# Three 256-column matmuls per weight tile, summed in one half bank of PSUM, in place of a 512-column and a 256-column one

## The chip, the cores and the metric

The kernel runs on one core of a Trainium2 chip. The metric is the device time of one execution in microseconds. The engines named below are PE (TensorE, matmuls; its weight loads have a row of their own, PEld), DVE (VectorE), ACT (ScalarE) and SP (SyncE, which here only issues DMAs). PSUM is the memory that PE writes: 8 banks of 512 fp32 columns on 128 partitions. SBUF is the memory that all engines read.

## What is computed

Two transformer-like blocks on one sequence of 256 tokens and width 2048, all in fp32:

```python
h = rmsnorm(x, g_mix)
z = h @ w_in                                  # cb, cc, cv, q, k, v, f, gate_c, gate_a
conv_y = cb * causal_dwconv(cc * cv, conv_w)
attn = forgetting_attention(q, k, v, log_f)   # 8 heads of 128
merged = sigmoid(gate_c + b) * (conv_y @ w_conv_out) + sigmoid(gate_a + b) * (attn @ w_attn_out)
x = x + merged @ w_mix_out
x = x + square(relu(rmsnorm(x, g_mlp) @ w_ff1)) @ w_ff2
x = rmsnorm(x, g_final)
# second block
q, k, v, p = split(rms_norm(x, g) @ w_in_2)
a = moba_attention(rms_norm(q), rms_norm(k), v, rel_bias)
m = multiscale_pool(p, pool_w, pool_scale)    # four products of 256 x 256
x = x + concat(a, m) @ w_out_2
x = x + (silu(gate) * val) @ w_down_2         # gate, val: conv(rms_norm(x) @ w_up_2)
```

With 256 tokens the work is the reading of 446 MB of weights and the matmuls on them.

## The kernel before, in words

**Precision.** Every fp32 operand of a large product is held as two numbers of type fp32r, a high part and the rest: a weight as WH and WL, an activation in a buffer of 16 K-blocks (XHL, MHL; AHL and CHL have 8) whose 512 columns are 256 tokens of high part, then 256 tokens of low part. A product is high x high + high x low + low x high.

**Weights** come by DMA in units of 1024 columns of 128 partitions (RAW, issued on SP), ACT rounds each to WH (L840), DVE subtracts to WL (L1279). There are five buffers of each, and both engines run up to four units ahead of PE.

**Items.** The program is one list of items that all engines walk in the same order. Three kinds matter here:

- *features* items (q, k, cc, cv, cb, the gates, conv, attn, ff, Q, K, pool, up gate, up val): the result has features on the partitions. The weight tile of 128 x 128 is the stationary operand and the activation the moving one. An item is 4 tiles wide and up to 16 K-blocks deep. For a K-block and a pair of tiles `j0`, `j0 + 1` PE does (L684) the two high weights against all 512 activation columns, then (L686) the two low weights against the 256 high columns. Each tile has a bank of its own: columns 0 to 255 collect high x high + low x high, columns 256 to 511 collect high x low.
- *tokens* items (v, the residual products) and *group* items (most of w_ff2 and w_down): the activation is stationary, the weight moves, three matmuls of 512 columns on one bank (`three`, L717 to L719). Groups have also seven-product steps (`sevens`), in which DVE builds sums of weights and activations.
- *small products* (transposes, scores, probabilities x values, head norms, row spreads, the two pooled products) are put between the parts of an item, at places written out by hand in the plan.

**PSUM.** The eight banks are two sides of four. Items take sides in turn; `take` makes PE wait until what was on the side has been read out. A small product goes to the side that the running item does not use, and is noted in the same `free` list.

**Evacuation.** A features item's two column halves are in PSUM; `fold` adds them: ACT copies the high x low half of all four banks to TA (L894), DVE adds the other half (L1363), and only then comes the step that the item is for, on TA: multiply by the row of norm factors RB (L1375, L1387, L1510, L1753, L1765) or by a gate. Each of these is a stage of a queue (`Pending`) that is pumped twice between two weight splits, so a stage stands behind a WH or WL split. Who may overwrite TA is kept in ACT's `free["TA"]`.

Of the kernel before, what the change touches and what calls it, by code (L numbers as in the profile page):

```python
# [5 lines left out]
P = 128  # L6
T = 256
# [83 lines left out]
class Part:  # L91
# [3 lines left out]
    banks: list  # L95
# [5 lines left out]
class Item:  # L101
# [4 lines left out]
    side: int = 0  # L106
    mid: dict = field(default_factory=dict)
# [5 lines left out]
    args: dict = field(default_factory=dict)  # L113

# [26 lines left out]
class Plan:  # L141
# [102 lines left out]
    def second_half(self):  # L244
# [12 lines left out]
        for i in range(2):  # L257
            at = POOL_AT[i]
            parts = self.tokens(w2, 0, ALLK[:at], 2048 + 512 * i)
            side = self.turn ^ 1  # L260
# [5 lines left out]
            small = Item("pooled", ("pooled", i), pool, ("M", "pools"), side, args={"i": i})  # L266
# [25 lines left out]
def build(nc, io):  # L292
# [5 lines left out]
    with ctx:  # L298
# [87 lines left out]
        def signals(names):  # L386
# [8 lines left out]
        hi, x_hi, part_hi, sum_hi, copied, squared, root, gate, tap, exps, probs, placed, softplus, cr_hi, pair1, rooted, act_step = (  # L395
            signals("hi x_hi part_hi sum_hi copied squared root gate tap exps probs placed softplus cr_hi pair1 rooted act_step"))

        lo, t_made, x_lo, summed, summing, left, evacuated, scaled, multiplied, tapped, mean, column, diagonal, row = (
            signals("lo t_made x_lo summed summing left evacuated scaled multiplied tapped mean column diagonal row"))
# [129 lines left out]
        def tensor(e):  # L529
# [3 lines left out]
            free = [None, None]  # L533

            def take(s):
                if free[s]:
                    own.wait_ge(*free[s][0][free[s][1]])
                return 4 * s

# [4 lines left out]
            def first(s, u):  # L544
# [11 lines left out]
                if u == 7:  # L556
                    free[1] = x_lo, ("mix", 15)

            def vec(s):
                b = take(s)  # L560
# [5 lines left out]
                free[s] = row_in, "vec"  # L566

            def rel(s):
                b = take(s)
                own.wait_ge(s_rel, rel_all)  # L570
                mm(PS[0:8, b, 0:384], RELT[:], OH[:, 0:384], start=True, stop=True).then_inc(*own.made(rel_up, "rel"))
                free[s] = row_in, "er"

            def spread(s, key):
                b = take(s)
# [4 lines left out]
                free[s] = row, key  # L580

            def log_f(s):
                b = take(s)
# [5 lines left out]
                free[s] = logit, "z"  # L589

            def running(s):
                b = take(s)
# [6 lines left out]
                free[s] = row_in, "cr"  # L599

            def score(s, block, h):
                b = take(s)
# [15 lines left out]
                free[s] = masked, (block, h)  # L618

            def turn(s, block, h):  # L620
                b = take(s)
# [5 lines left out]
                free[s] = probs, (block, h)  # L627

            def mix(s, block, h):
                vv, _ = ATT[block]  # L630
                b = take(s)
# [7 lines left out]
                free[s] = mixed, (block, h)  # L639

            def turn_x(s, of, g):
                b = take(s)
# [7 lines left out]
                free[s] = x_lo, (of, 4 * g + 3)  # L650

            def head_norm(s, key):
                sq = SQA if key[0] == "Q" else SQB
                b = take(s)
# [4 lines left out]
                free[s] = norm_left, key  # L659

            def pooled(s, it):
                features(it)

            small_products = {"first": first, "vec": vec, "rel": rel, "spread": spread, "log f": log_f, "running": running,
                              "scores": score, "turn": turn, "mix": mix, "turn x": turn_x, "head norm": head_norm,
                              "pooled": pooled}

            def between(it, n):
                for what, *args in it.mid.get(n, ()):
                    if what in small_products:  # L670
                        small_products[what](it.side ^ 1, *args)

            def features(it):
                b, x = take(it.side), BUF[it.src[0]]
                for n, p in enumerate(it.parts):
                    own.wait_ge(*lo[p.ent])
                    h, l = wview(WH, p.ent), wview(WL, p.ent)
                    for k, kc in enumerate(p.kcs):
# [3 lines left out]
                        for j0 in range(0, len(p.banks), 2):  # L682
                            for j in (j0, j0 + 1):
                                mm(PS[:, b + p.banks[j], :], h[:, k, j * P:(j + 1) * P], x[:, kc, :], start=st, stop=False)  # L684
                            for j in (j0, j0 + 1):
                                t = mm(PS[:, b + p.banks[j], 0:T], l[:, k, j * P:(j + 1) * P], x[:, kc, 0:T],  # L686
                                       start=False, stop=en)
                    t.then_inc(*own.made(used, p.ent))
                    between(it, n)
                free[it.side] = left, it.key  # L690

            def gates(it):
                b, (p,) = take(it.side), it.parts
# [4 lines left out]
                free[it.side] = evacuated, "f"  # L698

            def tokens(it):  # L700
                b, x = take(it.side), BUF[it.src[0]]
# [12 lines left out]
                free[it.side] = (placed, it.key) if it.kind == "v" else (evacuated, it.key)  # L714
# [6 lines left out]
            def group(it):  # L721
                b, x = take(it.side), MHL
                sevens = [n for n, st in enumerate(it.steps) if st.seven]
                for n, st in enumerate(it.steps):
# [22 lines left out]
                    if o:  # L747
                        bp = take(it.side ^ 1)
# [13 lines left out]
                    if c:  # L762
                        free[it.side ^ 1] = left, it.key
                last = {"out": (stored, (it.args["g"], 1, 1)), "final group": (evacuated, ("final", 1))}
                free[it.side] = last.get(it.kind, (evacuated, it.key))
# [6 lines left out]
            first(1, 0)  # L772
            zeros(WARM // 2)
            first(1, 1)
# [29 lines left out]
        ROW = {"proj": "r1", "cc": "r1", "cv": "r1", "cb": "r1", "gate": "r1", "ff": "r2", "qk": "r3", "pool": "r3"}  # L804
        SPREADS = [None, "r1", "r2", "r3", "r4"]
        SPREAD_SIDE = {args[0]: it.side ^ 1 for it in items for mids in it.mid.values() for what, *args in mids
# [6 lines left out]
        def wide_ps(it, lo_, hi_):  # L813
            return PS[:, 4 * it.side:4 * it.side + 4, lo_:hi_]

        def scalar(e):
# [71 lines left out]
            def fold(it):  # L888
                own.wait_ge(*used[it.end])
                if free["TA"]:  # L890
                    s, key = free["TA"]
                    own.wait_ge(*s[key])
                chain()
                e.copy(TA[:], wide_ps(it, T, 2 * T)).then_inc(*own.made(copied, it.key))  # L894
                yield
# [11 lines left out]
            def proj(it):  # L907
                yield from fold(it)
                free["TA"] = evacuated, it.key
# [16 lines left out]
            def running():  # L926
                own.wait_ge(*run_up["run"])
                b = 4 * (item_of["cc", 0].side ^ 1)
# [34 lines left out]
            def mix(s, block, h):  # L963
# [3 lines left out]
                act(dst[:, 4 * h:4 * h + 4, 0:T], PS[:, 4 * s:4 * s + 4, 0:T], AF.Copy).then_inc(  # L967
# [15 lines left out]
            def cc(it):  # L983
                yield from fold(it)
                free["TA"] = evacuated, it.key
                yield

            def cv(it):
                yield from fold(it)
                yield from nothing(2)  # L990
                free["TA"] = multiplied, it.key
                yield from taps(TB[:, :, 0:T], it.key, 4 * it.args["half"], False)

            def cb(it):
                yield from fold(it)
                yield from nothing(2)
                split_product(CHL, 4 * it.args["half"], it.key, multiplied)
                free["TA"] = evacuated, it.key

            def gates(it):  # L1000
                yield from fold(it)
                yield
                g, half = it.args["g"], it.args["half"]
                own.wait_ge(*scaled[it.key])
# [4 lines left out]
                free["TA"] = scaled, it.key  # L1009
                yield  # L1010

            def conv(it):
                yield from fold(it)
                free["TA"] = evacuated, it.key
                yield

            def attn(it):
                yield from fold(it)
                yield from nothing(2)
                split_product(MHL, 4 * it.args["g"], it.key, multiplied)  # L1020
                free["TA"] = evacuated, it.key

            def turn_x(s, of, g):
                for n in range(2):
                    if n == 0:
                        own.wait_ge(*turned[of, g])
                    split_bank(of, 4 * g + 2 * n, PS[:, 4 * s + n, :])
# [20 lines left out]
            def ff(it):  # L1048
                yield from fold(it)
# [897 lines left out]
```

## Time and profile before

| | us |
|---|---|
| median of 3 runs | 2383.57 (2383.52 to 2384.89) |
| the profiled execution | 2383.46 |
| its span, first to last instruction | 2381.6 |

| engine | busy us | share of the span | instructions |
|---|---|---|---|
| PE | 2376.9 | 100% | 12581 |
| PEld | 2035.4 | 85% | 12581 |
| DVE | 1700.7 | 71% | 1804 |
| ACT | 1216.5 | 51% | 1427 |

A matmul's recorded duration holds the time that it drains through the array, while the next already streams; what one costs in a row of them is the distance from its start to the next start, or its piece in the chain of waits. Each matmul has a weight load of its own, also where the stationary operand is that of the matmul before.

### The profile page before, as it was taken

To read this page: it belongs to the slowest core of one execution; us is meant where nothing else is said; L and a number is where in the kernel's file an instruction comes from. 1 tells how busy PE (TensorE), PEld (TensorE's weight loads), DVE (VectorE), ACT (ScalarE), POOL (GpSimd) and SP (SyncE) were. 2 spreads that over 40 slices of the span, in tenths; PEclk is the share of its full clock that TensorE was granted. 3 is DMA by queue.
4 is the path that set the end of the run, shared out by engine and by line. 5 is a ranking of instruction groups with operands and counts; after the bars stand their busy time and mean duration, and the time that the engine had idled before them with its cause. 6 is when DMAs were issued, how large, how long until landed. Compare 5 with 4: busy or idle time off the path is not lost.

```text
span 2381.6 us, 30785 instructions
## 1 busy us (share of the span) xinstructions
PE 2376.9 (100%) x12581; PEld 2035.4 (85%) x12581; DVE 1700.7 (71%) x1804; ACT 1216.5 (51%) x1427; POOL 0.2 (0%) x4
## 2 busy tenths in 40 slices
PE   9999999999999999999999999999999999999999
PEld 8888888888888888888888888888888888888887
DVE  6565666666568868868768667855778778886788
ACT  5444454554545445445445555555555455545554
POOL 0000000000000000000000000000000000000000
PEclk9999999999999999999999999999999999999999
DMA  7566556666555665655665565555655665566655
GB/s 253 160 187 196 167 185 196 191 188 196 186 187 178 219 216 189 213 181 198 202 190 193 182 185 160 171 183 186 186 181 194 196 192 176 186 219 186 188 173 181
DMA packets 238040, 452.15 MB, mean 190 GB/s; under 512 B 16569, under 2 KB 20779, under 8 KB 237771
## 3 DMA queue, kind: packets, MB, share of 16 engines
q1 hardware_dynamic: 237147, 449.07, 59.3%
q8 instruction: 99, 1.62, 0.3%
q10 hardware_dynamic: 752, 1.12, 0.1%
q14 instruction: 42, 0.34, 0.0%
HBM read 446.46 MB, written 3.67 MB: 189 GB/s over the span
## 4 chain that ended last, share of the span: by engine, by line
PE 97%; DVE 2%; ACT 0%; issue 0%; ACTq 0%; DVEq 0%
PE PS L684 41%; PE PS L686 21%; PE PS L717 11%; PE PS L718 11%; PE PS L719 11%; DVE WL L1279 1%; PE PS L648 0%; PE PS L615 0%; PE PS L636 0%; PE PS L657 0%; ACT WH L840 0%; PE PS L542 0%; PE PS L625 0%; DVE PB L1259 0%; PE PS L553 0%
## 5 line engine op out<-in xcount | busy, mean ns | idle before, releaser
L1279 DVE TENSOR_TENSOR WL<-RAW,WH 128x1024 fp32r<-128x1024 f32 (+1 forms) x844 | 1002.0, 1204 | 520.6 <-ACT WH L840 519.1
L684 PE MATMUL PS<-XHL,WH 128*128 128x512 f32 x3968 | 1248.9, 396 | 0.0
L840 ACT ACTIVATE WH<-RAW 128x1024 fp32r<-128x1024 f32 (+1 forms) x845 | 867.5, 1041 | 744.4 <-PE PS L686 478.3
L686 PEld LDWEIGHTS PS<-XHL,WL 128*128 128x128 f32 x3968 | 745.4, 188 | 176.0
L686 PE MATMUL PS<-XHL,WL 128*128 128x256 f32 x3968 | 779.7, 278 | 0.0
L684 PEld LDWEIGHTS PS<-XHL,WH 128*128 128x128 f32 x3968 | 605.1, 189 | 2.1 <-issue 1.0
L717 PE MATMUL PS<-WH,MHL 128*128 128x512 f32 x1000 | 390.2, 390 | 0.0
L719 PE MATMUL PS<-WH,MHL 128*128 128x512 f32 x1000 | 389.2, 389 | 0.0
L718 PE MATMUL PS<-WL,MHL 128*128 128x512 f32 x1000 | 389.1, 389 | 0.0
L719 PEld LDWEIGHTS PS<-WH,MHL 128*128 128x128 f32 x1000 | 187.7, 188 | 39.3
L717 PEld LDWEIGHTS PS<-WH,MHL 128*128 128x128 f32 x1000 | 187.7, 188 | 38.8 <-issue 0.3
L718 PEld LDWEIGHTS PS<-WL,MHL 128*128 128x128 f32 x1000 | 187.8, 188 | 38.0
L905 ACT ACTIVATE MHL<-TA 128x1024 fp32r<-128x1024 f32 x33 | 35.0, 1062 | 120.4 <-DVE TA L1600 61.9
L1363 DVE TENSOR_TENSOR TA<-TA,PS 128x1024 f32<-128x1024 f32 x72 | 87.9, 1221 | 3.7 <-ACT TA L894 1.2
L894 ACT COPY TA<-PS 128x1024 f32<-128x1024 f32 x72 | 73.3, 1018 | 13.5 <-DVE K L1694 3.3
L1380 DVE TENSOR_TENSOR MHL<-TA,MHL 128x1024 fp32r<-128x1024 f32 x33 | 40.5, 1226 | 28.0 <-ACT MHL L905 26.7
L840 ACT ACTIVATE WH<-PB 128x1024 fp32r<-128x1024 f32 x24 | 25.4, 1058 | 56.1 <-DVE PT L1271 43.6
L717 PE MATMUL PS<-WH,XHL 128*128 128x512 f32 x128 | 50.2, 392 | 0.0
L718 PE MATMUL PS<-WL,XHL 128*128 128x512 f32 x128 | 49.9, 390 | 0.0
L719 PE MATMUL PS<-WH,XHL 128*128 128x512 f32 x128 | 49.8, 389 | 0.0
L684 PE MATMUL PS<-AHL,WH 128*128 128x512 f32 x128 | 40.2, 395 | 0.0
L684 PE MATMUL PS<-CHL,WH 128*128 128x512 f32 x128 | 40.2, 395 | 0.0
(212 smaller groups left out, 1374.6 us busy)
## 6 DMA issues: line engine op xcount, KB each, us to landing
RAW<-in_w_ff SPq DMA_DIRECT2D x256, 512.0 KB, 4.1
RAW<-in_w_in SPq DMA_DIRECT2D x224, 512.0 KB, 3.9
RAW<-in_w_up SPq DMA_DIRECT2D x176, 512.0 KB, 4.1
RAW<-in_w_down SPq DMA_DIRECT2D x88, 512.0 KB, 4.4
RAW<-in_w_mix_out SPq DMA_DIRECT2D x32, 512.0 KB, 4.0
RAW<-in_w_out SPq DMA_DIRECT2D x32, 512.0 KB, 3.7
RAW<-in_w_conv_out SPq DMA_DIRECT2D x16, 512.0 KB, 3.7
RAW<-in_w_attn_out SPq DMA_DIRECT2D x16, 512.0 KB, 4.3
```

The costliest lines, as they stand in the source:

```text
L684: mm(PS[:, b + p.banks[j], :], h[:, k, j * P:(j + 1) * P], x[:, kc, :], start=st, stop=False)
L686: t = mm(PS[:, b + p.banks[j], 0:T], l[:, k, j * P:(j + 1) * P], x[:, kc, 0:T], start=False, stop=en)
L717: mm(PS[:, bank, :], xh, h, start=first, stop=False)
L718: mm(PS[:, bank, :], xh, l, start=False, stop=False)
L719: return mm(PS[:, bank, :], xl, h, start=False, stop=last)
L840: act(high, raw, AF.Copy).then_inc(*own.made(hi, i))
L894: e.copy(TA[:], wide_ps(it, T, 2 * T)).then_inc(*own.made(copied, it.key))
L905: act(dst[:, c0:c0 + 4, 0:T], TA[:], AF.Copy).then_inc(*own.made(part_hi, key))
L1279: tt(low, raw, high.bitcast(f32), sub).then_inc(*own.made(lo, i))
L1363: tt(TA[:], TA[:], wide_ps(it, 0, T), add).then_inc(*own.made(left, it.key))
L1380: tt(dst[:, c0:c0 + 4, T:2 * T], TA[:], dst[:, c0:c0 + 4, 0:T].bitcast(f32), sub).then_inc(*own.made(evacuated, key))
```

## The change

In features items each weight tile and K-block now has three matmuls of 256 columns on the same 256 columns of PSUM: high weight x high activation, high weight x low activation, low weight x high activation. The four tiles of an item are four quarters of two banks, so an item takes the first two banks of its side ("front"). The `start` flag stands at a bank's first quarter alone. `fold` is gone on ACT and DVE; the step that the item is for reads PSUM directly (`product`, `four`).

The other two banks of the side ("back") take the small products that are put into the item; scores and the transposes of the probabilities, which need four banks, stay on the other side. `take` becomes `front_of`, `back_of` and `all_of`, with a list each. `mix` packs its four heads into two banks. The pooled products go to the back banks of their own item, and are read from PSUM. ACT no longer writes TA at an item's start; where it does later (`up gate`, `up val`, `pool`, `head norm`) it waits first (`may_write_ta`). DVE gets one new wait: in the second gate item it waits for ACT's sigmoid of the first (`gate["gc", g]`) ahead of writing TA. DMAs, weight splits, tokens and group items keep their instructions.

```diff
@@ features, PE
-                b, x = take(it.side), BUF[it.src[0]]
+                b, x = (back_of(it.side) if it.base else front_of(it.side)), BUF[it.src[0]]
...
-                        for j0 in range(0, len(p.banks), 2):
-                            for j in (j0, j0 + 1):
-                                mm(PS[:, b + p.banks[j], :], h[:, k, j * P:(j + 1) * P], x[:, kc, :], start=st, stop=False)
-                            for j in (j0, j0 + 1):
-                                t = mm(PS[:, b + p.banks[j], 0:T], l[:, k, j * P:(j + 1) * P], x[:, kc, 0:T],
-                                       start=False, stop=en)
+                        for j, q in enumerate(p.quarters):
+                            o = PS[:, b + q // 2, T * (q % 2):T * (q % 2) + T]
+                            mm(o, h[:, k, j * P:(j + 1) * P], x[:, kc, 0:T], start=st and q % 2 == 0, stop=False)
+                            mm(o, h[:, k, j * P:(j + 1) * P], x[:, kc, T:2 * T], start=False, stop=False)
+                            t = mm(o, l[:, k, j * P:(j + 1) * P], x[:, kc, 0:T], start=False, stop=en and q % 2 == 1)
...
-                free[it.side] = left, it.key
+                if it.kind == "pooled":
+                    back[it.side] = pool_in, 4 * it.args["i"] + 3
+                else:
+                    front[it.side] = OUT_OF_PSUM.get(it.kind, left), it.key
@@ fold, ACT
-                e.copy(TA[:], wide_ps(it, T, 2 * T)).then_inc(*own.made(copied, it.key))
@@ fold, DVE
-                tt(TA[:], TA[:], wide_ps(it, 0, T), add).then_inc(*own.made(left, it.key))
+            def product(it):
+                chain()
+                own.wait_ge(*used[it.end])
+                return four(it.bank)
@@ up val, DVE
-                yield from fold(it)
-                chain()
-                tt(TC[:, :, 2:258], TA[:], over4(RB[:]), mul).then_inc(*own.made(multiplied, it.key))
+                tt(TC[:, :, 2:258], product(it), over4(RB[:]), mul).then_inc(*own.made(multiplied, it.key))
@@ gates, DVE
+                if it.args["half"]:
+                    own.wait_ge(*gate["gc", it.args["g"]])
@@ mix, PE
-                    mm(PS[:, b + i, 0:T], vv[:, 0, c:c + P], PT[:, i, 0:T], start=True, stop=False)
-                    t = mm(PS[:, b + i, P:T], vv[:, 1, c:c + P], PT[:, i, T:384], start=False, stop=True)
+                    o = PS[:, b + i // 2, T * (i % 2):T * (i % 2) + T]
+                    mm(o, vv[:, 0, c:c + P], PT[:, i, 0:T], start=True, stop=False)
+                    t = mm(o[:, P:T], vv[:, 1, c:c + P], PT[:, i, T:384], start=False, stop=True)
```

PE's instructions around the transposes of the first attention's probabilities (L625 before, L638 after; both are `turn`, PB the probabilities, CONST the identity), before:

```order
L684 MATMUL PS<-XHL,WH 128x512 x2
L686 MATMUL PS<-XHL,WL 128x256 x2
L625 MATMUL PS<-CONST,PB 128x128 x12
L684 MATMUL PS<-XHL,WH 128x512 x2
L686 MATMUL PS<-XHL,WL 128x256 x2
```

and after the change:

```order
L703 MATMUL PS<-XHL,WL 128x256
L638 MATMUL PS<-CONST,PB 128x128 x12
L701 MATMUL PS<-XHL,WH 128x256
L702 MATMUL PS<-XHL,WH 128x256
L703 MATMUL PS<-XHL,WL 128x256
L701 MATMUL PS<-XHL,WH 128x256
L702 MATMUL PS<-XHL,WH 128x256
```

Four matmuls for two tiles (1536 columns) become six (1536 columns); the small product stands at the same place.

DVE at the last `up val` item, ahead of the seven-product step of the last group; L1363 is the fold, L1765 the multiplication by RB, L1497 and L1503 the convolution's taps, L1259 to L1271 the weight sums of the seven-product step. Before:

```order
L1363 TENSOR_TENSOR TA<-TA,PS 128x1024
L1765 TENSOR_TENSOR TC<-TA,RB 128x4x256
L1279 TENSOR_TENSOR WL<-RAW,WH 128x1024
L1497 SCALAR_TENSOR_TENSOR TA<-TC,VEC,TA 128x256 x4
L1279 TENSOR_TENSOR WL<-RAW,WH 128x1024
L1503 SCALAR_TENSOR_TENSOR TA<-TC,VEC,TA 128x256 x4
L1769 TENSOR_TENSOR TA<-TA,TB 128x1024
```

and after:

```order
L1279 TENSOR_TENSOR WL<-RAW,WH 128x1024 x6
L1750 TENSOR_TENSOR TC<-PS,RB 128x4x256
L1279 TENSOR_TENSOR WL<-RAW,WH 128x1024
L1496 SCALAR_TENSOR_TENSOR TA<-TC,VEC,TA 128x256 x4
L1502 SCALAR_TENSOR_TENSOR TA<-TC,VEC,TA 128x256 x4
L1279 TENSOR_TENSOR WL<-RAW,WH 128x1024
L1754 TENSOR_TENSOR TA<-TA,TB 128x1024
```

One instruction of 1024 columns is gone and the multiplication reads PSUM; one weight split has moved from between the taps to behind them.

## Rows read from the trace of the kernel before

**Rows 1.** The page: engines' busy time, and their busy tenths over time.

```profile
PE 2376.9 (100%) x12581; PEld 2035.4 (85%) x12581; DVE 1700.7 (71%) x1804; ACT 1216.5 (51%) x1427; POOL 0.2 (0%) x4
...
PEclk9999999999999999999999999999999999999999
```

**Rows 2.** The page's chain that ended last: shares of the span.

```profile
PE 97%; DVE 2%; ACT 0%; issue 0%; ACTq 0%; DVEq 0%
```

**Rows 3.** Groups by line and shape: count | busy us, mean ns | idle before.

```profile
L684 PE MATMUL PS<-XHL,WH 128*128 128x512 f32 x3968 | 1248.9, 396 | 0.0
...
L1363 DVE TENSOR_TENSOR TA<-TA,PS 128x1024 f32<-128x1024 f32 x72 | 87.9, 1221 | 3.7 <-ACT TA L894 1.2
L894 ACT COPY TA<-PS 128x1024 f32<-128x1024 f32 x72 | 73.3, 1018 | 13.5 <-DVE K L1694 3.3 <-DVE Q L1694 2.5 <-DVE MHL L1380 2.5
...
L684 PE MATMUL PS<-AHL,WH 128*128 128x512 f32 x128 | 40.2, 395 | 0.0
...
L684 PE MATMUL PS<-CHL,WH 128*128 128x512 f32 x128 | 40.2, 395 | 0.0
...
L684 PE MATMUL PS<-MHL,WH 128*128 128x512 f32 x16 | 5.0, 394 | 0.0
```

**Rows 4.** Chain that ended last, 300 to 480 us: share of the stretch by line.

```profile
by line: PE PS L684 67.0%; PE PS L686 33.1%
```

**Rows 5.** The same stretch: busy us (count), of L686, then of L684 alone.

```profile
300.00:480.00 180.00, 101.45 (x517) 97.15 (x518) 1.00 0.62 192
...
300.00:480.00 180.00, 162.31 (x518) 1.00 0.62 192
```

**Rows 6.** Weight loads of features items in order of time: start us, us.

```profile
900.37 0.42 PEld L686 LDWEIGHTS PS<-XHL,WL 128*128 128x128 f32 x2
900.72 0.30 PEld L684 LDWEIGHTS PS<-XHL,WH 128*128 128x128 f32 x2
```

**Rows 7.** Chain pieces in features items and a `mix` block: start us, us.

```profile
152.05 0.43 PE PS L636 x2
152.49 0.22 PE PS L637 x2
152.71 0.46 PE PS L684 x2
153.17 0.23 PE PS L686 x2
```

**Rows 8.** Longest chain pieces: runs of one kind of matmul: start us, us.

```profile
58.45 3.71 PE PS L696 x16
...
132.04 1.31 PE PS L625 x12
```

**Rows 9.** Chain shares in a group item, 2330 to 2370 us, then L718's count.

```profile
by line: PE PS L717 33.5%; PE PS L719 33.5%; PE PS L718 33.4%
...
2330.00:2370.00 40.00, 22.95 (x59) 10.96 (x60) 1.00 0.57 192
```

**Rows 10.** Who the weight loads waited for: us in total, times, longest.

```profile
PEld PS L717 <- DVE WL L1279: 1.1, 2, 0.6
...
PEld PS L717 <- DVE TA L1363: 0.5, 1, 0.5
```

**Rows 11.** PE matmuls, then weight loads, at one such wait: start us, us.

```profile
2080.88 0.39 PE L719 MATMUL PS<-WH,AXL 128*128 128x512 f32 x1
2081.38 0.50 PE L717 MATMUL PS<-WH,AXH 128*128 128x512 f32 x1
...
2081.94 0.39 PE L719 MATMUL PS<-WH,AXL 128*128 128x512 f32 x1
...
2081.38 0.19 PEld L717 LDWEIGHTS PS<-WH,AXH 128*128 128x128 f32 x1 [0.54 <-DVE WL L1279]
2081.48 0.19 PEld L718 LDWEIGHTS PS<-WL,AXH 128*128 128x128 f32 x1
```

**Rows 12.** DVE before that wait and at 61 us: start us, us.

```profile
2055.14 1.22 DVE L1363 TENSOR_TENSOR TA<-TA,PS 128x1024 f32<-128x1024 f32 x1
...
60.90 1.22 DVE L1363 TENSOR_TENSOR TA<-TA,PS 128x1024 f32<-128x1024 f32 x1
```

More of the change, by code:

```diff
@@ L113, with bank @@
     args: dict = field(default_factory=dict)
+    @property
+    def bank(self):
+        return 4 * self.side + self.base
     @property
@@ L556, in first @@
                 if u == 7:
-                    free[1] = x_lo, ("mix", 15)
+                    front[1] = back[1] = x_lo, ("mix", 15)
             def vec(s):
-                b = take(s)
+                b = back_of(s)
                 own.wait_ge(s_const, 16)
@@ L579, in spread @@
                 t.then_inc(*own.made(spread_up, key))
-                free[s] = row, key
+                back[s] = row, key
             def log_f(s):
-                b = take(s)
+                b = back_of(s)
                 own.wait_ge(*evacuated["f"])
@@ L617, in score @@
                 t.then_inc(*own.made(scores, (block, h)))
-                free[s] = masked, (block, h)
+                front[s] = back[s] = masked, (block, h)
             def turn(s, block, h):
-                b = take(s)
+                b = all_of(s)
                 own.wait_ge(*normed["P", block, h])
@@ L626, in turn @@
                 t.then_inc(*own.made(probs_up, (block, h)))
-                free[s] = probs, (block, h)
+                front[s] = back[s] = probs, (block, h)
             def mix(s, block, h):
                 vv, _ = ATT[block]
-                b = take(s)
+                b = back_of(s)
                 own.wait_ge(*probs[block, h])
@@ L713, in tokens @@
                     between(it, i)
-                free[it.side] = (placed, it.key) if it.kind == "v" else (evacuated, it.key)
+                front[it.side] = (placed, it.key) if it.kind == "v" else (evacuated, it.key)
             def three(bank, xh, xl, h, l, first, last):
@@ L762, in group @@
                     if c:
-                        free[it.side ^ 1] = left, it.key
+                        front[it.side ^ 1] = back[it.side ^ 1] = left, it.key
                 last = {"out": (stored, (it.args["g"], 1, 1)), "final group": (evacuated, ("final", 1))}
-                free[it.side] = last.get(it.kind, (evacuated, it.key))
+                front[it.side] = back[it.side] = last.get(it.kind, (evacuated, it.key))
             own.wait_ge(*zero_made["zero"])
@@ L886, in columns2, with may_write_ta, fresh @@
                 yield
[L888 to L892, printed above, removed]
-                chain()
-                e.copy(TA[:], wide_ps(it, T, 2 * T)).then_inc(*own.made(copied, it.key))
-                yield
+            def may_write_ta():
+                s, key = free["TA"]
+                own.wait_ge(*s[key])
+            def fresh(it):
                 if it.key in FRESH:
@@ L1086, in qk @@
             def qk(it):
-                yield from fold(it)
-                free["TA"] = evacuated, it.key
+                yield from fresh(it)
                 yield
@@ L1201, in parts @@
                             work.flush()
-                            g = pooled(args[0])
-                            next(g)
-                            work.later(g)
+                            work.later(pooled(args[0]))
             free["EV"] = None
@@ L1762, in up_val @@
                 g = it.args["g"]
-                yield from fold(it)
-                chain()
-                tt(TC[:, :, 2:258], TA[:], over4(RB[:]), mul).then_inc(*own.made(multiplied, it.key))
+                tt(TC[:, :, 2:258], product(it), over4(RB[:]), mul).then_inc(*own.made(multiplied, it.key))
                 yield
@@ L1828, in parts @@
                             work.flush()
[L1829 to L1831 removed]
+                            work.later(pooled(args[0]))
             e.memset(ZERO, 0.0).then_inc(*own.made(zero_made, "zero"))
```

248 lines of the change are left out of this document (112 added, 136 removed).

## The prediction

> **What bounds the kernel now.** I read the page first. PE is busy all through the span at the full granted clock, while DVE has 29% and ACT 49% of it to spare [rows 1], and the chain that ended last is 97% matmuls [rows 2]. So the time is the sum of what each matmul takes of PE's stream, plus the few places where PE waits. What one takes is not its recorded 396 ns [rows 3], which counts the drain too; it is the piece that it has in the chain. I took a stretch of 180 us that holds features items alone. There the 512-column matmuls are 67.0% of the chain and the 256-column ones 33.1% [rows 4], with 518 and 517 of them [rows 5]: 0.670 x 180 / 518 = 232.8 ns and 0.331 x 180 / 517 = 115.24 ns. The single pieces agree: 0.46 and 0.23 us for two [rows 7]. A weight tile and K-block costs one of each, 348.06 ns. There are 3968 + 128 + 128 + 16 = 4240 of them [rows 3], 1476 us of the span.
>
> **The matmuls.** The change takes away 4240 matmuls of 512 columns and adds 8480 of 256. The columns stay the same, 768 for a tile and K-block; matmuls and weight loads grow from two to three. If each of the three takes what the 256-column ones take now, a tile and K-block costs 3 x 115.24 = 345.7 ns, 2.34 less, and all of them 2.34 x 4240 = 9.9 us less. The shares are rounded to 0.1%, which is up to 0.5 ns here, so 2 us either way.
>
> Why should a 256-column matmul keep its 115 ns when no long ones stand around it? Three things could end that.
>
> Weight loads: a load starts together with the matmul ahead of it, not earlier. Two loads that stand beside 256-column matmuls fit into 0.30 us although each lasts 0.19, so the second begins some 0.11 us behind the first [rows 6]. After a stall two loads of the same kind start 0.10 us apart [rows 11]. The load is therefore no longer than the 115 ns that it has to hide under, and since none is drawn further ahead now, the present pairs of 256s are already in the state in which all would be: of the four loads of a pair of tiles, two lie under a 256-column matmul. The bound from below is the run of 12 transposes, each with a load of its own: 1.31 / 12 = 109 ns [rows 8]. The bound from above comes from the group items, below (120.5 ns). I take 115.24, since it is the same instruction on the same buffers.
>
> PSUM: three matmuls in a row now add to the same 256 columns, 115 ns apart; before, neighbours were on different banks. In `mix`, the second matmul of each head adds to the columns that the first wrote 0.43 / 2 / 2 = 0.11 us earlier, and it takes 0.22 / 2 = 0.11 us, as a transpose of 128 columns does [rows 7, 8]. Nothing for it, then. If the adder did stall, each matmul would show more than 115 ns, which is the same rival as the next.
>
> Instructions: PE gets two (load, matmul) in 115 ns, without a pause. The longest run at such a rate is 12 pairs [rows 8], so whether the supply holds for 192 pairs of a whole item isn't shown. Nothing for it, with the price in the rival.
>
> **The fold.** 72 copies of 1.018 us on ACT and 72 additions of 1.221 us on DVE [rows 3]. 73 and 88 us leave two engines that are not the bound, so all of it is hidden except where PE waits for them. The multiplication that now reads PSUM is of the same 1024 columns as the addition that read PSUM (1.22 us), and takes that one's place in the queue. PE waited three times for a DVE result for over 0.3 us: twice for a weight sum's low part in a seven-product step, once for the fold itself [rows 10]. At the first of the two, three matmuls took 2081.94 - 2080.88 = 1.06 us in place of 3 x 0.227 = 0.68, so 0.38 us are lost [rows 11]; DVE's chain up to there had begun with a fold at 2055.14 [rows 12]. A chain shorter by 1.2 us removes a wait of 0.38: 2 x 0.38 = 0.8 us less. What is late next there is the landing and splitting of the units behind, for which I have no row and count nothing. The third, at the first v item, stays: DVE did the fold at 60.90, behind other work [rows 12], and will do k's multiplication at that moment.
>
> **PSUM sides and waits.** A features item's front is free when its first read of PSUM is done; that is one DVE instruction after the item's end, before it was a copy and an addition, and the side is wanted only an item later (22 us for 16 K-blocks). Small products in the back banks wait for the small product before them, where they used to wait for an evacuation as well. `scores` and the transposes still wait for the other side, whose item ended at least two parts earlier. Bounds: no gain, since no row shows PE waiting there; no loss, since each wait is for something no later than before. Zero. The new wait on DVE (second gate item, for a sigmoid of the item before): behind it are DVE's weight splits, for which PE waits; but the sigmoids come a whole item earlier. Zero. The pooled products lose a fold: hidden.
>
> **A rule against the change.** The rows give 232.8 ns for 512 columns and 115.24 for 256, so more than twice for twice the columns, no fixed cost per matmul. The Trainium skill, page "TensorE: Matmul & The Clock Gate", section "Back-to-back issue gap", gives columns / 2.4 + 2.5 ns for a warm matmul, a small fixed cost: by it a third matmul is 2.5 ns more for each tile and K-block, an estimate of 10.6 us more in all, 2394 us. The same rule would put the present pair at 325 ns, where the rows have 348.
>
> **The sum.** 2383.46 (the profiled execution; the median of the runs is 2383.57) - 9.9 - 0.8 = 2372.8 us, 0.45% less.
>
> **Rivals.**
>
> *Each matmul costs a fixed amount (slower).* In a group item a 512-column matmul takes 0.335 x 40 / 59 = 227.1 ns [rows 9]. At 2.4 GHz 512 columns stream in 213.3, which leaves 13.8. In features items 348.06 - 320 = 28.1 for two matmuls, 14.0 each: nearly the same, which speaks for a cost per matmul, paid somewhere in the pair and not where the starts show it. Then a 256-column matmul costs 106.7 + 13.8 = 120.5 ns, three cost 361.4, 13.3 more, and the kernel takes 2383.46 + 56.6 - 0.8 = 2439 us. Against it: the starts in features items are 0.23 us apart for two 256s and 0.46 for two 512s, every time, and 16 matmuls of 512 columns with a stationary operand of only 16 columns still take 3.71 / 16 = 232 ns each [rows 8], so the rate seems to belong to the columns that stream. The point at which it decides is 116.0 ns a matmul (348.06 / 3), not one ns above what I count on. A supply of instructions that doesn't keep up, or a stall in PSUM's adder, ends here too. Chance 0.22, anywhere from 2388 to 2440.
>
> *Staying on one bank is quicker (faster than forecast).* Groups stay on a bank for three matmuls and have 227.1 ns, features change banks and have 232.8. If that is the cause, 256 columns cost 115.24 x 227.1 / 232.8 = 112.4 ns, three 337.3, and the kernel takes 2383.46 - 45.8 - 0.8 = 2337 us. At the transposes' 109 ns it would be 2383.46 - 86.8 - 0.8 = 2296. Against it: the 16 matmuls just named are on one bank and have 232. Chance 0.10.
>
> *Nothing changes.* The two weight loads of the same tile may weigh as the long matmul did, or the 256s come out at 115.5 to 116.5 ns instead of 115.24: 2379 to 2388 us. The forecast is only 2.34 ns a tile, so a small error in it lands here. Chance 0.13.
>
> **Chances.** The forecast's own case, 114.6 to 115.5 ns a matmul, 2364 to 2379 us: 0.55. A measurement here can tell about 0.2%, 4.8 us. Faster by more: 0.55 + 0.10 = 0.65, less 0.04 for its upper edge, 0.61. Slower by more: 0.22. The rest, 0.17, is no change. A range from 2355 to 2440 leaves out the quicker case, 0.10, and what little would be above 2440.
>
> **What the profile after would show.** In a stretch of features items the three lines have a third of the chain each, 115 ns a matmul, and the stretch of an item of 16 K-blocks is 22.1 us. Over 116.0 ns, and evenly on all three lines, is the fixed cost. More on the second and third line than on the first is PSUM's adder. Weight loads that start later than their matmul's predecessor would show the instruction supply. ACT's busy time falls to 1143 us, DVE's to 1613; the waits for L1279's weight sums are gone. I am wrong if PE waits at item starts or small products for a bank, or if the group and tokens items, which nothing touches, change their 227 ns.

## Result: 2438.17 us, 2.3% slower

| | before | after |
|---|---|---|
| median of runs, us | 2383.55 | 2438.17 (2437.67 to 2438.70, 4 runs) |
| ratio | | 1.0228, 95% interval 1.021 to 1.0246 |
| span of the profiled execution | 2381.6 | 2436.8 |
| granted clock | full | full |

I had forecast 2372.8 us. The change costs 54.6 us where I counted on a gain of 11. The rival "each matmul costs a fixed amount" had 2439 us.

The page of the changed kernel, in answer to [rows 1] and [rows 2]:

```profile
PE 2427.0 (100%) x16821; PEld 2273.0 (93%) x16821; DVE 1616.5 (66%) x1732; ACT 1142.7 (47%) x1355; POOL 0.2 (0%) x4
...
PE 96%; DVE 2%; ACT 1%; issue 0%; DMA 0%; ACTq 0%; DVEq 0%
```

PE has 4240 matmuls and 4240 loads more. ACT has lost what was forecast (1143 us), DVE nearly (1613). Together they have 3% of the chain, so the gain on them is worth next to nothing.

The chain of waits in a stretch of features items alone, 310 to 480 us, and the count of L701 there (L702 and L703 have 473 too), in answer to [rows 4] and [rows 5]:

```profile
by line: PE PS L703 33.4%; PE PS L701 33.4%; PE PS L702 33.3%
...
310.00:480.00 170.00, 133.66 (x473) 1.00 0.59 182
```

0.334 x 170 / 473 = 120.0 ns for each of the three lines, where I had counted on 115.24. A tile and K-block takes 360 ns and not 345.7. In order of time, PE's matmuls and then its weight loads (start us, us; compare [rows 6]):

```profile
400.01 0.28 PE L702 MATMUL PS<-XHL,WH 128*128 128x256 f32 x1
400.13 0.28 PE L703 MATMUL PS<-XHL,WL 128*128 128x256 f32 x1
400.25 0.28 PE L701 MATMUL PS<-XHL,WH 128*128 128x256 f32 x1
...
400.02 0.19 PEld L703 LDWEIGHTS PS<-XHL,WL 128*128 128x128 f32 x1
400.14 0.19 PEld L701 LDWEIGHTS PS<-XHL,WH 128*128 128x128 f32 x1
400.26 0.19 PEld L702 LDWEIGHTS PS<-XHL,WH 128*128 128x128 f32 x1
```

Some 98% of the starts in features items are exactly 120 ns behind the one before, on all three lines alike. The group items have kept their 227 ns.

The extra 11.9 ns (360 - 348.06) on 4240 tiles and K-blocks are 50.6 us. The rest, some 4 us, is waiting: by the starts, PE now stands five times, together 5.3 us longer than ordinary steps, where it stood twice for 0.6 us together. Who the weight loads and the matmuls waited for (us, times, longest), in answer to [rows 10]:

```profile
PEld PS L736 <- DVE WL L1279: 2.2, 3, 1.2
...
PE PS L701 <- DVE WL L1279: 2.8, 2, 1.4
```

I had said that the waits for L1279 would be gone; there are five of them now where there were two, and longer ones. The first, in order of time (compare [rows 11]):

```profile
2050.99 0.28 PE L703 MATMUL PS<-XHL,WL 128*128 128x256 f32 x1
2052.68 0.35 PE L701 MATMUL PS<-XHL,WH 128*128 128x256 f32 x1 [1.41 <-DVE WL L1279]
```

1.69 us from start to start where a step is 0.12.

### The profile page after: what moved, and what is told of

Read it like the earlier page. It is cut to its first block, busy times and chain, and to the rows that moved or that the text cites. A ratio compares the mean times of both kernels' runs of the same rounds, so it can differ in the third digit from the quotient of the medians.

```text
span 2436.8 us, 39061 instructions
## 1 busy us (share of the span) xinstructions
PE 2427.0 (100%) x16821; PEld 2273.0 (93%) x16821; DVE 1616.5 (66%) x1732; ACT 1142.7 (47%) x1355; POOL 0.2 (0%) x4
## 4 chain that ended last, share of the span: by engine, by line
PE 96%; DVE 2%; ACT 1%; issue 0%; DMA 0%; ACTq 0%; DVEq 0%
PE PS L701 20%; PE PS L703 20%; PE PS L702 20%; PE PS L736 11%; PE PS L738 11%; PE PS L737 11%; DVE WL L1279 1%; PE PS L662 0%; ACT WH L862 0%; PE PS L628 0%; PE PS L650 0%; PE PS L671 0%; PE PS L638 0%; ACT TA L994 0%; DVE TA L1502 0%
## 5 line engine op out<-in xcount | busy, mean ns | idle before, releaser
L1279 DVE TENSOR_TENSOR WL<-RAW,WH 128x1024 fp32r<-128x1024 f32 (+1 forms) x844 | 1002.4, 1205 | 690.6 <-ACT WH L862 688.0
L862 ACT ACTIVATE WH<-RAW 128x1024 fp32r<-128x1024 f32 (+1 forms) x845 | 865.3, 1041 | 859.4 <-PE PS L703 569.3
L701 PE MATMUL PS<-XHL,WH 128*128 128x256 f32 x3968 | 1125.8, 284 | 2.8 <-DVE WL L1279 2.8
L703 PE MATMUL PS<-XHL,WL 128*128 128x256 f32 x3968 | 1122.8, 283 | 0.0
L702 PE MATMUL PS<-XHL,WH 128*128 128x256 f32 x3968 | 1122.8, 283 | 0.0
L701 PEld LDWEIGHTS PS<-XHL,WH 128*128 128x128 f32 x3968 | 761.5, 192 | 4.6 <-issue 4.0
L702 PEld LDWEIGHTS PS<-XHL,WH 128*128 128x128 f32 x3968 | 761.6, 192 | 0.5
L703 PEld LDWEIGHTS PS<-XHL,WL 128*128 128x128 f32 x3968 | 761.5, 192 | 0.0
L924 ACT ACTIVATE MHL<-TA 128x1024 fp32r<-128x1024 f32 x33 | 35.0, 1061 | 99.8 <-DVE TA L1754 65.6
L862 ACT ACTIVATE WH<-PB 128x1024 fp32r<-128x1024 f32 x24 | 25.4, 1059 | 56.0 <-DVE PT L1271 43.5
L736 PE MATMUL PS<-WH,AXH 128*128 128x512 f32 x96 | 37.7, 393 | 1.1 <-DVE WL L1279 1.1
L994 ACT ACTIVATE TB<-TC,VEC 128x256 f32<-128x256 f32 x44 | 22.9, 591 | 32.7 <-DVE TC L1740 32.7
```

Of the source, the lines that this page charges most:

```text
L701: mm(o, h[:, k, j * P:(j + 1) * P], x[:, kc, 0:T], start=st and q % 2 == 0, stop=False)
L702: mm(o, h[:, k, j * P:(j + 1) * P], x[:, kc, T:2 * T], start=False, stop=False)
L703: t = mm(o, l[:, k, j * P:(j + 1) * P], x[:, kc, 0:T], start=False, stop=en and q % 2 == 1)
L736: mm(PS[:, bank, :], xh, h, start=first, stop=False)
L862: act(high, raw, AF.Copy).then_inc(*own.made(hi, i))
L924: act(dst[:, c0:c0 + 4, 0:T], TA[:], AF.Copy).then_inc(*own.made(part_hi, key))
```

## Experiments

Theory F: a matmul on fp32r operands costs its columns at 2.4 GHz and a fixed 13 to 14 ns, so the third matmul is what the change costs; the 233 and 115 ns between starts before the change don't show the cost of each. Theory S: what waiting there is comes from the stage that went with the fold (a stage is one entry of the queue that ACT and DVE work off between two weight splits). Times of single executions are compared with 2383.5 to 2383.7 us of the kernel before on the same chip. "Per tile" below is ns of one weight tile and one K-block, from the starts in the trace with the small joints at the ends of items in it (before: 348.5, after: 360.5 when counted so).

### Only the split, in the kernel before

```diff
-                                mm(PS[:, b + p.banks[j], :], h[:, k, j * P:(j + 1) * P], x[:, kc, :], start=st, stop=False)
+                                w = h[:, k, j * P:(j + 1) * P]
+                                mm(PS[:, b + p.banks[j], 0:T], w, x[:, kc, 0:T], start=st, stop=False)
+                                mm(PS[:, b + p.banks[j], T:2 * T], w, x[:, kc, T:2 * T], start=False, stop=False)
```

> The kernel before, with one edit: each 512-column matmul of a features item becomes two of 256 columns, on the same bank and the same columns as before. Fold, banks and sides stay as before. Theory F (each matmul costs its columns at 2.4 GHz and some 13.5 ns more, whatever its length): all 256-column matmuls are 120 ns apart, a tile and K-block goes from 348 to 360 ns, and the time from 2383.5 to about 2433 us. Rival P (the changed kernel is slow because three matmuls in a row add to the same PSUM columns): here only two of them are on the same columns and not in a row, so they keep 115 ns and the time is 2373 us. Rival R (something else in the change, evacuation or banks, slows PE): 2383 us or less.

2432.5 us, 48.9 more than before. Its page and its chain from 320 to 480 us:

```profile
PE 2424.9 (100%) x16821; PEld 2271.5 (93%) x16821; DVE 1701.3 (70%) x1804; ACT 1217.4 (50%) x1427; POOL 0.2 (0%) x4
...
by line: PE PS L686 33.4%; PE PS L685 33.4%; PE PS L688 33.3%
```

DVE and ACT still have the fold, four banks are in use, no three matmuls in a row are on the same columns, and the three lines have a third of the chain each, at 120 ns. This one edit holds 48.9 of the 54.6 us. P and R are out.

### Two banks in turns, in the changed kernel

```diff
+                            for c in range(2):
+                                for w, lo_ in ((h, 0), (h, T), (l, 0)):
+                                    for q in (c, c + 2):
...
+                                        t = mm(o, w[:, k, q * P:(q + 1) * P], x[:, kc, lo_:lo_ + T],
```

> The changed kernel, with the matmuls of two tiles taken in turns (tile q and q + 2, whose quarters lie in different banks), so that no matmul adds to the columns of the one before it. Same matmuls, same sums. Theory F: 120 ns a matmul still, 2438 us. Rival P (PSUM's adder on the same columns): back to about 115 ns, 3 x 5 x 4240 = 64 us less, 2375 us.

2437.5 us, 120 ns. Adding to the columns of the matmul before costs nothing that shows, and loading the same tile twice in a row (here there is another between) isn't what costs either.

### Runs of eight, in the kernel before

```diff
-                        for j0 in range(0, len(p.banks), 2):
-                            for j in (j0, j0 + 1):
-                                mm(PS[:, b + p.banks[j], :], h[:, k, j * P:(j + 1) * P], x[:, kc, :], start=st, stop=False)
-                            for j in (j0, j0 + 1):
-                                t = mm(PS[:, b + p.banks[j], 0:T], l[:, k, j * P:(j + 1) * P], x[:, kc, 0:T],
...
+                    for k, kc in enumerate(p.kcs):
+                        for j, bank in enumerate(p.banks):
+                            mm(PS[:, b + bank, :], h[:, k, j * P:(j + 1) * P], x[:, kc, :],
...
+                    for k, kc in enumerate(p.kcs):
+                        for j, bank in enumerate(p.banks):
+                            t = mm(PS[:, b + bank, 0:T], l[:, k, j * P:(j + 1) * P], x[:, kc, 0:T],
...
```

> The kernel before, with the matmuls of a unit (two K-blocks, four tiles) in another order: eight of 512 columns, then eight of 256, where it had two and two. Same matmuls. Theory F: the time stays at 2383.5 us within 3 us (16 matmuls still take 2787 ns); and if the starts only show a shifted picture of a fixed cost, the later ones of the run of eight are 227 ns (512 columns) and 120 ns (256 columns) apart, not 233 and 115. Rival C (the cost lies in the columns, 232.8 and 115.2 ns, and something else makes 120 of it in the changed kernel): 233 and 115 ns all through both runs.

2387.9 us, 4.2 more; per tile 349.3. The chain's pieces (start us, us):

```profile
400.24 0.95 PE PS L687 x8
401.19 1.84 PE PS L683 x8
403.03 0.95 PE PS L687 x8
```

0.95 / 8 = 119 and 1.84 / 8 = 230 ns, not 115 and 233. By the starts, the mean over some 530 such runs, without those behind a small product: the eight of 512 columns are 233, 235, 229, 232, 231, 227, 227, 227 ns apart, the eight of 256 columns 113, 119, and then 120 six times. So the 115 ns of the kernel before were about the mean of the first and second short one behind a long one, and the 233 that of the first long ones behind a short one. Settled, they are 120 and 227. This is the run that shows where I went wrong: same matmuls, same columns, only the row is longer.

### 128 moving columns

```diff
-                            mm(o, h[:, k, j * P:(j + 1) * P], x[:, kc, T:2 * T], start=False, stop=False)
-                            t = mm(o, l[:, k, j * P:(j + 1) * P], x[:, kc, 0:T], start=False, stop=en and q % 2 == 1)
+                            mm(o[:, 0:P], h[:, k, j * P:(j + 1) * P], x[:, kc, T:T + P], start=False, stop=False)
+                            t = mm(o[:, 0:P], l[:, k, j * P:(j + 1) * P], x[:, kc, 0:P], start=False, stop=en and q % 2 == 1)
```

> The changed kernel, with the second and third matmul of each tile and K-block on 128 columns instead of 256 (the low parts of tokens 128 to 255 are left out; the weight loads are all there). Theory F: 53.3 + 13.5 = 67 ns each for these two, 254 ns for a tile and K-block, 106 less than 360, and 450 us less in all: 1990 us, if the weights come fast enough. Rival L (the changed kernel is bound by its weight loads, or by the supply of instructions, at 120 ns each): nothing changes, 2438 us. Rival L109 (loads bound at the transposes' 109 ns): 120 + 109 + 109 = 338 ns, 2345 us.

2411.5 us. A third of the columns less brings 27 us, not 450. The weight loads (start us, us), in a stretch at the full granted clock:

```profile
399.90 0.19 PEld L703 LDWEIGHTS PS<-XHL,WL 128*128 128x128 f32 x1
400.01 0.19 PEld L701 LDWEIGHTS PS<-XHL,WH 128*128 128x128 f32 x1
400.12 0.19 PEld L702 LDWEIGHTS PS<-XHL,WH 128*128 128x128 f32 x1
400.24 0.19 PEld L703 LDWEIGHTS PS<-XHL,WL 128*128 128x128 f32 x1
```

The matmuls start 168, 59 and 113 ns apart, the loads more evenly, 109 to 120: 340 ns for the three, 113 each. So F as I wrote it, with no lower bound, is wrong below 256 columns: a pair of load and matmul has a floor of 113 ns. None of the three lengths I gave for it was right (67, 120, 109); it is between the last two.

340 in place of 360.5 ns would be 87 us less, and the whole kernel gained 27. Most of the difference is the clock. PEclk of the page, PE's starts around the first of its two longest pauses, and the count of matmuls in 60 us at the lower clock (after it: granted clock, DMA share, GB/s):

```profile
PEclk9999999999999999999999999999999995899979
...
1977.00 0.28 PE L703 MATMUL PS<-XHL,WL 128*128 128x128 f32 x1
1979.95 0.36 PE L701 MATMUL PS<-XHL,WH 128*128 128x256 f32 x1 [2.68 <-DVE WL L1279]
...
1990.00:2050.00 60.00, 60.00 (x283) 0.50 0.36 110
```

PE stood for 2.95 us from start to start at 1977 and again at 2277, each time waiting for a weight split. The granted clock was 0.50, the level of 1.2 GHz, from 1981 to 2063 us and from 2282 to 2323. There a tile and K-block took 640 ns in place of 340; some 180 of them were in the two stretches, 55 us. The time can't be used as it stands, the distances can.

### Fewer weight columns

```diff
-                            mm(o, h[:, k, j * P:(j + 1) * P], x[:, kc, T:2 * T], start=False, stop=False)
-                            t = mm(o, l[:, k, j * P:(j + 1) * P], x[:, kc, 0:T], start=False, stop=en and q % 2 == 1)
+                            m = P if en else 64
+                            mm(o[0:m], h[:, k, j * P:j * P + m], x[:, kc, T:2 * T], start=False, stop=False)
+                            t = mm(o[0:m], l[:, k, j * P:j * P + m], x[:, kc, 0:T], start=False, stop=en and q % 2 == 1)
```

> The changed kernel, with weight loads of 64 columns instead of 128 for the second and third matmul of each tile and K-block (their products for 64 of the 128 features are left out, except at an item's last K-block); the moving side keeps its 256 columns. Theory F (120 ns = 256 columns at 2.4 GHz + 13.3 ns per matmul, not bound by the load's length): 120 ns all the same, 2438 us. Rival L (with 256 columns the load's length is the bound): matmuls whose load is short come 109 to 115 ns after their predecessor; two of three at 112 would be 16 ns less for a tile and K-block, 68 us in all, 2370 us.

2408.9 us, per tile 353.4, that is 117.8 ns a matmul: between the two. The width of a load counts at 256 moving columns, but for a fifth of the fixed part (2.4 of 13.3 ns, as a mean of the three matmuls), and it is not the bound that I had as a rival. The next two were to say how it counts.

With 32 columns:

```diff
-                            m = P if en else 64
+                            m = P if en else 32
```

> The changed kernel, with weight loads of 32 columns instead of 128 for the second and third matmul of each tile and K-block (products for 96 of the 128 features left out, except at an item's last K-block). Theory D (proportional): 192 columns less of loads, at 7.5 ns for 128: 11.2 ns less than 360, 348.8 ns, 2391 us. Rival B (the load counts only as a bound, and at 64 columns it is already below the stream): 352.5 ns, 2409 us, as with 64 columns.

2410.6 us, per tile 353.9. Half the load again brings nothing, so not proportional: rival B, as far as this goes.

In the three matmuls of 512 columns of tokens and group items, in the kernel before:

```diff
+                m = P if last else 64
                 mm(PS[:, bank, :], xh, h, start=first, stop=False)
-                mm(PS[:, bank, :], xh, l, start=False, stop=False)
-                return mm(PS[:, bank, :], xl, h, start=False, stop=last)
+                mm(PS[0:m, bank, :], xh[:, 0:m], l, start=False, stop=False)
+                return mm(PS[0:m, bank, :], xl[:, 0:m], h, start=False, stop=last)
```

> The kernel before, with stationary operands of 64 columns instead of 128 in the second and third matmul of each three of the tokens and group items (their products for 64 of the 128 tokens are left out, except at an accumulation's end); the moving side keeps its 512 columns. Features items are untouched. In the run with 64-column weights a tile and K-block went from 360 to 352.5 ns, 3.7 ns for each load of 64 columns less. Theory D (a load takes from the stream in proportion to what it loads, also under a long matmul): 227 ns become 223, 2448 matmuls, 9 us less, 2374 us. Rival B (a load's length counts only where it is near the bound, at 256 columns): 227 ns and 2383.6 us, since a load of 0.19 us is well hidden under 0.227.

2391.9 us, 8.4 more. Both expectations miss, and the sign is against me: with shorter loads these matmuls are 229.4 ns apart on average, by the starts, where they had 227. Narrow loads don't speed the stream at 512 columns, they slow it. The gate item of the kernel before fits in: its 16 matmuls of 512 columns have a stationary operand of 16 columns and 232 ns each, and don't come down to 227 in a row of 16. So 128, 64 (in two of three) and 16 stationary columns have 227, 229.4 and 232 ns. I have no cause for it that the runs show.

### Other orders of the same matmuls

In the kernel before, one long and one short in turns:

```diff
-                        for j0 in range(0, len(p.banks), 2):
-                            for j in (j0, j0 + 1):
...
+                        for j, bank in enumerate(p.banks):
+                            mm(PS[:, b + bank, :], h[:, k, j * P:(j + 1) * P], x[:, kc, :], start=st, stop=False)
+                            t = mm(PS[:, b + bank, 0:T], l[:, k, j * P:(j + 1) * P], x[:, kc, 0:T], start=False, stop=en)
```

and four and four, which has the line `for j, bank in enumerate(p.banks):` a second time ahead of the last one:

> The kernel before, with the two matmuls of a tile in turns: 512, 256, 512, 256 columns, where it had 512, 512, 256, 256. Same matmuls. In the runs of eight, the first 256-column matmul after a 512 had 113 ns and the first 512 after a 256 had 233, which sum to 346. Theory F (a matmul's fixed cost is paid whatever the order; the starts only shift it): 347 to 349 ns for a tile and K-block, 2378 to 2387 us. Rival O (a 256-column matmul between long ones is really cheaper, as 113 ns): 340 to 346 ns, 2374 us or less.

> The kernel before, with four matmuls of 512 columns, then four of 256 in each K-block. A tile and K-block takes 348.4 ns in twos, 350.5 in turns (one and one), 349.1 in eights. Theory T (what a change of length costs falls with fewer changes, what a run of short ones costs is the settled 120): 348 to 349 ns, 2382 to 2387 us. Rival: fours are a better mix than both, 347 ns (227 + 120), 2378 us, which would be quicker than the kernel before.

In turns: 2392.3 us, 8.6 more (ratio 1.0036, 1.002 to 1.0052), per tile 350.6. Fours: 2393.1 us, 9.6 more (1.0041, 1.0021 to 1.006), per tile 350.8. With the twos at 348.5 and the eights at 349.3 there is no trend with the number of changes, so theory T of the fours fails, and so does "a short one between long ones is really cheaper". Where the lengths alternate or go in fours the short ones are 116 to 119 ns and the long ones 232 to 234. The kernel before has the best of the four orders by 0.8 to 2.3 ns a tile; why is open.

### One stage put back, in the changed kernel

```diff
@@ up gate and up val, ACT and DVE
+                yield
```

> The changed kernel, with one empty stage put back where the fold's stage stood, in the up gate and up val items of the second block, on ACT and DVE alike: nothing is computed more or less, the later stages stand one stage later between the weight splits, as before the change. Theory S (the five long waits of PE, 5.3 us beyond a normal step, come from ACT standing at the high split of the up val product ahead of a weight split): these waits go, 2433 us. Rival M (they come from what was left out or moved elsewhere, the direct reading of PSUM or the waits on TA): 2438 us as the changed kernel.

2431.6 us, 6.5 less than the changed kernel's 2438.17. Of PE's waits for L1279 none is left; the list of its matmuls' waits is:

```profile
PE PS L555 <- DVE SQ L1820: 1.0, 1, 1.0
PE PS L790 <- DMA VR<-in_g_mix: 0.2, 1, 0.2
```

ACT's instructions where the first of the long waits was (L1050 rounds the activation sums for the seven-product steps, L862 is the high split of a weight), in the changed kernel:

```order
L862 ACTIVATE WH<-RAW 128x1024
L1050 ACTIVATE AXH<-AS 128x512 x2
L862 ACTIVATE WH<-RAW 128x1024 x5
```

and with the stage put back:

```order
L1050 ACTIVATE AXH<-AS 128x512
L862 ACTIVATE WH<-RAW 128x1024
L1050 ACTIVATE AXH<-AS 128x512
L862 ACTIVATE WH<-RAW 128x1024 x5
```

With the fold's stage gone, both roundings stand in a row, and each waits for sums on DVE. ACT in the changed kernel there (start us, us, [idle before, releaser]):

```profile
2041.95 1.06 ACT L924 ACTIVATE MHL<-TA 128x1024 fp32r<-128x1024 f32 x1 [5.96 <-DVE TA L1754]
2042.92 1.04 ACT L862 ACTIVATE WH<-RAW 128x1024 fp32r<-128x1024 f32 x1
2046.87 0.63 ACT L1050 ACTIVATE AXH<-AS 128x512 fp32r<-128x512 f32 x1 [2.91 <-DVE AS L1581]
2049.70 0.63 ACT L1050 ACTIVATE AXH<-AS 128x512 fp32r<-128x512 f32 x1 [2.20 <-DVE AS L1581]
2050.24 3.88 ACT L862 ACTIVATE WH<-RAW 128x1024 fp32r<-128x1024 f32 x4
```

From 2036 to 2050 ACT made one weight split. The next five stood behind the sums and came in a burst (the view ends within the fifth), and PE lost 1.6 us. The second long wait, at 2321 us, has the same picture: ACT waits 5.97 us at L924, then 2.91 and 2.19 at the two roundings. The three in the last group, from 2372 us on, come after a third wait of 5.97 us at L924, with no rounding of activation sums behind it; I did not follow those further. That all five depend on the stage is what the run shows. Theory S holds, with the instruction named slightly wrong: I had said the high split of the product (L924) alone. Its wait for DVE's product went from 65.6 us in 11 times (longest 6.0) to 22.2 (longest 2.3).

## Why the prediction was wrong

**What bounds the kernel**: right. PE's stream sets the time, and its length was the sum of the matmuls.

**The matmuls**: this is the step that failed. I took 232.8 and 115.24 ns from the chain of waits and counted them as the costs of the two kinds. Their sum for a pair is a fact, and it was 348; the division did not give the price of each, because each distance holds something of its neighbour. The sentence that went wrong is "the present pairs of 256s are already in the state in which all would be". The runs of eight show that this state needs a third short one in a row: 113, 119, then 120. The forecast hung on a difference of 2.34 ns that was smaller than the 5 ns which the neighbours move.

The right division stood in the rows: 14.0 ns over the bare columns for each of two matmuls in features items, 13.8 for each in groups. I worked it out, called it "nearly the same, which speaks for a cost per matmul", and gave it 0.22. I weighed it down by the starts 0.23 and 0.46 us apart, the very figures in question, and by the run of 16 matmuls with 232 ns. That run was no witness: it has narrow stationary operands, and the run with 64 of them shows that narrow ones are slower at 512 columns. The rival's price was 120.5 ns and 2439 us; 120.0 and 2438 were measured. That its time is met within 1 us is in part luck: its matmuls were to cost 56.6 us more and cost 50.6, and it had 0.8 us less waiting where there were some 4 us more.

The settled distances give the cost as a line: 227 ns for 512 columns, 120 for 256, so 107 for 256 columns (256 / 2.4 = 106.7) and 13.3 on top of each. What the 13.3 ns are made of stays open: each matmul has a load of its own in all these runs, and none could part the two. The rule of the Trainium skill that I set against the change (page "TensorE: Matmul & The Clock Gate", section "Back-to-back issue gap") has this form and the right sign; its fixed part of 2.5 ns is too small for these fp32r matmuls, so 2394 us was too low. The plain fp32 matmuls of this kernel do come near it. The head norms, recorded twice each, in the chain of the kernel before (start us, us; the transposes are in [rows 8]):

```profile
1399.14 1.73 PE PS L657 x8
```

1.73 / 8 = 216 ns for 256 columns, and 1.31 / 12 = 109 for the transposes' 128: 107 ns for 128 columns, twice what fp32r takes, and 2 to 3 ns on top. So the small fixed cost belongs to the fp32 ones in this trace and the large one to the fp32r ones. It also suggests that the transposes' 109 ns were the time of their columns, and not that of a load as I had taken it; no run tells the two apart.

**PSUM's adder**: right, nothing (two banks in turns). **Weight loads as a bound**: right that a load of 128 columns fits under 120 ns, wrong in that the floor is the 109 ns of the transposes; it is 113 for these. **Instruction supply**: nothing was seen of it at 120 ns; in the changed kernel each load starts 2 to 3 ns behind the matmul before its own all through.

**The fold**: that 161 us of ACT and DVE work are hidden was right, and the split alone, with the fold in place, shows it: 2432.5 us with it, 2431.6 without it (and with the stage put back). That a shorter DVE chain would remove 0.8 us of waits was wrong by sign. I looked at the length of the chain and not at the order: a stage that goes moves all later stages of the item against the weight splits. I had written the order of DVE at such a place into the list of the change, and not asked what moves on ACT. It cost some 5 us by the starts and 6.5 by the run with the stage put back. That the third wait would stay was right (0.6 us, now for DVE's K).

**Sides, new waits, pooled products**: zero, as forecast; no such wait is among those of PE or its loads.

**The range** held the time, since it reached to this rival; the direction was wrong, and no part of the gain that I forecast came.

## What to carry to other kernels

Distances between starts in a mixed row are not prices. Where a change makes a row of one kind out of a mixed one, take the price from a place where that kind already stands in a long row, and check it against the sum of the mixed row under both divisions. With the columns unchanged, fewer and longer fp32r matmuls are cheaper, here by 13.3 ns each in settled rows and by 12 in the row of before. And when a stage is taken out of a queue that interleaves with something PE waits for, write down the new order on every engine of the queue, not only its length.

## What the runs showed of the hardware

- A weight load and an fp32r matmul in a settled row: 120 ns with 256 columns, 227 with 512, and 113 on average where two of three have 128.
- Plain fp32 matmuls: 216 ns for 256 columns and 109 for 128, 2 to 3 ns above twice the columns' time at 2.4 GHz; fp32r ones are 13.3 ns above the columns' time.
- Behind a long matmul the first short one is followed after 113 ns, the second after 119, and from the third on it is 120 ns; in a row of long ones behind a short one, 227 is reached with the sixth.
- A third matmul that adds to the PSUM columns of the one before it costs nothing that shows: 2437.5 us without such neighbours, 2438.2 with them.
- At the granted clock of 0.50 the tile of 256, 128 and 128 columns took 640 ns in place of 340.
- Four orders of the same 16 matmuls differ by 2.3 ns in 350 a tile: twos 348.5, eights 349.3, turns 350.6, fours 350.8. Unexplained.
- Weight loads narrowed to 64 columns in two of three matmuls brought 2.4 ns a matmul at 256 moving columns, narrowed to 32 no more than that (2.2 ns), and at 512 moving columns 64 cost 2.5 ns. Unexplained.
